# Splitting the turning of gathered rows between VectorE and TensorE, five column groups to three instead of four to four

## The reference

```python
def hmoe(x, p):
    """Two-level routing per token: top-1 expert group, then top-2 experts inside it."""
    t = x.reshape(bsz * L, D_MODEL)
    ...
    combine = jnp.einsum("tk,tke->te", gates,
                         jax.nn.one_hot(expert_id, N_EXPERTS, dtype=f32)).astype(x.dtype)
    out = jnp.zeros_like(t)
    for e in range(N_EXPERTS):
        hid = jax.nn.silu(t @ p["w_gate"][e]) * (t @ p["w_up"][e])
        out = out + (hid @ p["w_down"][e]) * combine[:, e:e + 1]
    return out.reshape(bsz, L, D_MODEL)
```

## Time and profile before

| | |
|---|---|
| median of 3 runs | 845.36 us (845.11 to 846.49) |
| the profiled execution | 845.81 us |
| span of the profiled execution, first to last instruction | 844.1 us |
| PE busy / PE weight loads busy | 789.7 / 647.9 us |
| DVE busy | 467.5 us (55%) |
| ACT busy / POOL busy | 204.4 / 104.5 us |
| mean granted TensorE clock | 0.976 of full speed |
| HBM read / written | 156.80 MB / 17.88 MB |

### The profile page before, as it was taken

The page is one execution under the profiler, slowest core; times in us unless marked ns, Lnnn a source line. Parts: engine busy times, 40 slices in busy tenths (PEclk is TensorE's granted clock), DMA queues, the critical chain, the costliest instruction groups (busy, mean ns, idle before and its releaser), DMA issues. The chain is left out here.

```text
span 844.1 us, 21325 instructions
## 1 busy us (share of the span) xinstructions
PE 789.7 (94%) x8993; PEld 647.9 (77%) x8993; DVE 467.5 (55%) x1092; ACT 204.4 (24%) x457; POOL 104.5 (12%) x169
## 2 busy tenths in 40 slices
PE   5999999999999999999999999698999999999935
PEld 3778877877888888777888888676778788788722
DVE  5999987236540242401223444756677777777726
ACT  5102325443211000102222211222222222222203
POOL 1000100113210000000000000122223223223100
PEclk9999999999999999999999989599999999999978
DMA  9531351131124900511021330799999999999745
GB/s 327 216 83 31 57 201 50 54 105 59 50 82 161 391 3 1 197 53 50 1 101 75 111 140 26 265 407 393 386 397 407 394 391 393 396 391 390 284 135 228
DMA packets 43654, 166.30 MB, mean 197 GB/s; under 512 B 16336, under 2 KB 21328, under 8 KB 26768
## 3 DMA queue, kind: packets, MB, share of 16 engines
q1 hardware_dynamic: 32912, 150.36, 47.1%
q0 software_dynamic: 6144, 9.45, 3.4%
q10 hardware_dynamic: 4544, 5.73, 1.9%
HBM read 156.80 MB, written 17.88 MB: 207 GB/s over the span
## 5 line engine op out<-in xcount | busy, mean ns | idle before, releaser
L876 PE MATMUL bank<-act_a,weight_ring 128*128 128x288 f32 x640 | 157.3, 406 | 0.5 <-ACT act_a L1436 0.5
L2300 DVE STREAM_TRANSPOSE region_t<-region_r 32x128 f32<-32x128 f32 x372 | 151.3, 407 | 6.8 <-DMA region_r<-ffn_rows,gather_now 0.7
L876 PEld LDWEIGHTS bank<-act_a,weight_ring 128*128 128x128 f32 x640 | 120.9, 190 | 33.3 <-ACT act_a L1436 0.6
L1164 PE MATMUL bank<-weight_ring,act_b 128*128 128x256 f32 x512 | 114.2, 385 | 0.0
L1164 PEld LDWEIGHTS bank<-weight_ring,act_b 128*128 128x128 f32 x512 | 98.5, 193 | 13.6
L1754 DVE TENSOR_TENSOR region_u<-region_u,bank 128x512 f32<-128x512 f32 (+1 forms) x26 | 17.9, 687 | 92.7 <-PE bank L1164 70.1
L1360 PE MATMUL bank<-region_t,weight_ring 128*64 128x80 f32 x1536 | 56.9, 233 | 1.9 <-issue 1.4
L1360 PEld LDWEIGHTS bank<-region_t,weight_ring 128*64 128x64 f32 x1536 | 54.6, 139 | 5.2 <-issue 4.5
L2262 DVE TENSOR_REDUCE score_max<-bank 128x2 f32<-128x512 f32 (+1 forms) x10 | 6.4, 637 | 65.3 <-PE bank L1204 61.5
L1360 PEld LDWEIGHTS bank<-region_t,region_g 128*64 128x64 f32 x1024 | 37.1, 138 | 6.6 <-issue 6.6
L1360 PE MATMUL bank<-region_t,region_g 128*64 128x80 f32 x1024 | 39.5, 234 | 2.7 <-issue 2.7
(11 more groups left out here) (355 smaller groups left out, 1178.8 us busy)
## 6 DMA issues: line engine op xcount, KB each, us to landing
weight_ring<-in_w_chunks SPq DMA_DIRECT2D x28, 1024.0 KB, 7.9
weight_ring<-in_w_up SPq DMA_DIRECT2D x17, 1024.0 KB, 11.8
weight_ring<-in_w_down SPq DMA_DIRECT2D x10, 1024.0 KB, 11.3
region_g<-in_w_up SPq DMA_DIRECT2D x8, 1024.0 KB, 12.2
region_g<-in_w_gate SPq DMA_DIRECT2D x8, 1024.0 KB, 9.7
conv_io<-in_w_gate SPq DMA_DIRECT2D x8, 1024.0 KB
conv_io<-in_w_down SPq DMA_DIRECT2D x8, 1024.0 KB, 11.5
weight_ring<-in_w_gate SPq DMA_DIRECT2D x7, 1024.0 KB
```

The lines of the kernel that those rows point to most:

```text
L876: m = pe.matmul(ps[:, 0:HALF], slot(c)[:, k, P * (mt % 2):P * (mt % 2 + 1)], x[:, k, HALF * h:HALF * (h + 1)], start=(k == 0), stop=(k == ...
L1164: m = pe.matmul(ps[0:L, CW * cc:CW * (cc + 1)], x[:, k, t0:t0 + L], slot(c)[:, k, :], start=(k == 0), stop=(k == KD - 1))
L2300: m = dve.transpose(xgT[b][DB * part:DB * (part + 1), 0:4, DB * blk:DB * (blk + 1)], xg[b][DB * blk:DB * (blk + 1), CW * part:CW * (part + 1)]
```

## The change

A constant `BY_DVE` takes the place of the fixed four: VectorE turns groups 0 to 4 and PE groups 5 to 7. The number of VectorE's instructions stays the same, each has five blocks instead of four; PE does three transposes instead of four for each expert, and ScalarE copies three groups. For the first expert PE still turns eight groups, three for ScalarE's copy and five for VectorE's.

```diff
+BY_DVE = 5
...
             def turn_x(pp, b):
 
                 pe.wait_ge(gathered[b], 16 * pp + 16)
-                for k in range(4):
-                    m = turn(banks[b][:, CAP * k:CAP * (k + 1)], xg[b][0:CAP, 4 + k::KD])
+                for k in range(KD - BY_DVE):
+                    m = turn(banks[b][:, CAP * k:CAP * (k + 1)], xg[b][0:CAP, BY_DVE + k::KD])
                 m.then_inc(turned_x, 1)
 
             def turn_first(pp, p):
 
                 turn_x(pp, 0)
-                for k in range(4):
+                for k in range(BY_DVE):
                     m = turn(banks[1][:, CAP * k:CAP * (k + 1)], xg[0][0:CAP, k::KD])
                 m.then_inc(first_turned, 1)
...
             def copy_x(pp, b):
 
                 act.wait_ge(turned_x, 2 * pp + (b + 1))
-                act.activation(xgT[b][:, 4:8, 0:CAP], banks[b][:, 0:4 * CAP].rearrange("p (k l) -> p k l", k=4), ACT.Copy)\
+                act.activation(xgT[b][:, BY_DVE:KD, 0:CAP],
+                               banks[b][:, 0:(KD - BY_DVE) * CAP].rearrange("p (k l) -> p k l", k=KD - BY_DVE), ACT.Copy)\
                     .then_inc(xT_act, 1)
...
                 for part in (2 * half, 2 * half + 1):
                     for blk in range(3):
                         m = dve.transpose(
-                            xgT[b][DB * part:DB * (part + 1), 0:4, DB * blk:DB * (blk + 1)],
+                            xgT[b][DB * part:DB * (part + 1), 0:BY_DVE, DB * blk:DB * (blk + 1)],
                             xg[b][DB * blk:DB * (blk + 1), CW * part:CW * (part + 1)]
-                            .rearrange("p (c k) -> p k c", k=KD)[:, 0:4])
+                            .rearrange("p (c k) -> p k c", k=KD)[:, 0:BY_DVE])
                 if half == 1:
                     m.then_inc(xT_dve, 1)
 
             def copy_first(p):
 
                 dve.wait_ge(first_turned, p + 1)
-                dve.tensor_copy(xgT[0][:, 0:4, 0:CAP], banks[1][:, 0:4 * CAP].rearrange("p (k l) -> p k l", k=4))\
+                dve.tensor_copy(xgT[0][:, 0:BY_DVE, 0:CAP],
+                                banks[1][:, 0:BY_DVE * CAP].rearrange("p (k l) -> p k l", k=BY_DVE))\
                     .then_inc(xT_dve, 1)
```

## The result

The changed kernel takes 851.39 us (median of 7 runs, 848.30 to 854.49), the kernel before 846.49 us (7 runs, 845.11 to 847.83): a ratio of 1.0058, 95% interval 1.0036 to 1.0080. It is slower, and by more than was forecast (847.8 us); the median lies 0.7 us above the range's upper end.

The account below looks back on a forecast made before the run. PE and its waits set the pace until 795 us, with DVE's turning path to become the bound; 3.0 + 0.08 - 0.68 = +2.4 us on the median of 845.36 gave 847.8 us (+0.28%), range 845.1 to 850.7.

Parts of the forecast that it names:

- What bounds the kernel: Expert stage: until 795 us PE and what it waits for set the pace, with a period of 7.91 us.
- 0.23 us of slack on DVE's: Between hidden product and next gate: DVE's path would allow the gate at 672.84, but it begins at 673.07.
- Its signs: Changed profile: turning 465 to 470 ns, distance 2.95 us, idle time labelled region_t, no in_w_up wait, period 8.04.
- The turning's 60 ns: DVE's turning instruction, 407 ns for 128 elements, takes 60 ns more for 160; six lie before the gate, 0.36 us.
- block nearly free: Rival on DVE's turning instruction: the extra block costs only 33 to 50 ns, time 845.4 to 846.4; chance 0.22.
- The first expert's +0.08 us: Ahead of the first gate: DVE's copy from PSUM is one group larger, +0.08 us.
- PE's transpose is worth 0.04 us: Before the down product: one transpose less gains 0.04 us, not 0.15, because PE then waits for the hidden product.
- So +0.13 us in 23 places, 3.0 us; in the seven others 2.95 is still under 3.08, nothing.: Hidden product to gate: 2.95 us instead of 2.82 in 23 places; the seven where PE's loop starts keep 3.08.
- - 0.68: Up product of expert 30: PE arrives 2.9 us later, so its 0.68 us delay for the weight goes away.
- The base: The kernel before: the forecast's +2.4 us was added to its median of 845.36 us.
- in proportion: Rival on DVE's turning: it grows by 80 to 102 ns and up, 854.4 us at 102 ns; chance 0.12.
- Faster through the transfers: Rival: PE reaches the 592 to 600 us transfer hole sooner, at most -0.7 us, if DVE's path doesn't bind; chance 0.06.

Follow-up runs that it names:

- seven to five: The change with DVE's twelve turning instructions dealt seven ahead of the hidden product and five behind it, instead of six and six: 845.83 us, ratio 0.9988.
- the two sizes of the experiments: The changed kernel with BY_DVE = 6 (860.94 us, 1.0180) and with BY_DVE = 3 (847.25 us, 1.0015).
- DVE's part alone: Against the kernel before, DVE turns five groups while PE still transposes four, group 4 left unread in the bank: 850.89 us, 1.0037.
- six groups: The changed kernel with BY_DVE = 6, so DVE turns six groups and PE two: 860.94 us, 1.0180 against the kernel before.
- filled end: Unread PE products added in the wait before the final sum; with 14, the kernel before takes 844.37 us, the change 848.01 us.
- 34 products: 34 unread PE products added in the wait before the final sum: the kernel before takes 861.35 us, the change 864.23 us.
- seven to five with 34: The change with turning dealt seven ahead and five behind, plus 34 unread PE products before the final sum: 862.07 us, 1.0173.
- eight to four: The change with DVE's turning instructions dealt eight ahead of the hidden product and four behind it: 849.70 us, 1.0032.

## Why the prediction was wrong, step by step

*What bounds the kernel.* Right. The distance from hidden product to gate is the longer of two paths, and 0.23 us of slack on DVE's was right: at five groups the gate follows the turning by 0.07 us, at four (with PE's transpose gone) and at seven to five it doesn't. Its signs came, but for two: the idle time ahead of the gate is labelled "issue" and not `region_t`, and the plain period is 8.07 us (671.18 to 679.25 from hidden product to hidden product) instead of 8.04.

*The turning's 60 ns.* Right: 467 ns. With the two sizes of the experiments it is 348, 407, 467 and 525 ns for three to six blocks, 59 ns for each, and some 170 ns that don't grow. These rows have 1.85 ns an element, nearly twice the 1.04 ns of plain work, with a source read at a stride of eight. The rival of a block nearly free, at 33 ns, is refuted. The Trainium skill, "Vector Engine (DVE) Microarchitecture Reference", section 3.8, has one element per cycle and lane in transposing; the measured instruction does not keep to that pace. Whether the stride is the reason was not tried.

*The first expert's +0.08 us.* Right for the copy, which takes 0.57 us instead of 0.49; in the time it can't be seen.

*PE's transpose is worth 0.04 us.* Right: 0.04 by the timeline, 1.1 us or nothing by the medians, and in the change not even that, since DVE is later (DVE's part alone takes as long as the whole).

*"So +0.13 us in 23 places, 3.0 us; in the seven others 2.95 is still under 3.08, nothing."* This is the step that failed, in its size: the 0.06 us between turning and gate were taken for every place. The seven loop starts stayed (but for one, with 3.17 instead of 3.08), and 16 places grew by 0.13 to 0.14. But seven of the 23, the fourth expert of each turn of the loop, grew by 0.25: 16 x 0.135 + 7 x 0.25 = 3.9 us. There the gate follows the turning by 0.19 us instead of 0.07. The kernel before could not show it: there PE wasn't waiting for DVE. DVE's part alone (3.07 to 3.08) and six groups (3.40 to 3.44, against 3.30) have it too, seven to five doesn't (2.78). With six groups the loop starts have it as well, so it goes with PE being released late by DVE at the last expert ahead of the loop's branch or the first one behind it; why it costs 0.12 us there is open.

The 22 experts from 6 to 28 give the size without the noise: +3.2 us. They hold 17 of the 23 places, for which the forecast had 17 x 0.13 = 2.2. Of the 1.0 that is missing 0.6 are the five fourth experts among them; the rest is small things: 0.1 at the loop starts, 0.1 in the plain places, and 0.2 between gate and hidden product (4.78 us instead of 4.77).

*"- 0.68" for the weight's wait.* The wait is gone in the changed kernel, as forecast. But it isn't a fixed property of the kernel before. Over five profiles of kernels with four groups on either engine it was 0.7, 0.6 and 0.3 us, and twice nothing. With the stall in the first experts, which also varies, one pair of profiles says little: the stage took 254.57, 254.17, 252.92 and 253.79 us in four profiles of the kernel before with and without filled end (mean 253.9), and 257.33, 257.37, 257.85 and 256.35 in four of the change alike (mean 257.2; the profile with 34 products, 259.47, is left out, see below). That is +3.4 us, against the forecast's 3.0 - 0.7 = 2.3. The difference is the seven fourth experts, 0.8, and the wait, which was on average smaller than 0.68 (0.3 over the five profiles).

*The base.* The forecast stood on 845.36 us, the median of three runs. The kernel before has had 846.49, 846.87, 845.75, 847.02 and 846.77 over 7 to 35 runs. Against the 846.8 of the two longest series the forecast of +2.4 would have read 849.2. The change has 850.4 to 851.4. So of the 3.6 us between forecast and result about 1.4 were the base, 1.1 the stage (3.4 against 2.3), and the rest is within the scatter of the medians.

*What the range left out.* The end. Nothing in the argument let it vary, and the profiles show 37.6 to 41.3 us for it. It did not decide the sign. Whether it adds to the median of the change is open: the profiles of the change are 848.9 to 849.7 us long and the two of the kernel before 844.1 and 842.6, a difference of 6.0, while medians differ by 3.6 to 4.9. The profiled executions of the kernel before, 845.81 and 844.36 us, lie in the lower half of its own spread (842.17 to 850.9 over 35 runs).

*The rivals.* "Nearly free" and "in proportion" fall by the 467 ns. "Faster through the transfers" had its condition right (DVE's path must not bind), and seven to five fulfils it: 0.9988 with the weight's wait back in the profile. By the interval it is still no gain over the kernel before.

## What to carry to other kernels

Between two engines that release each other, what counts is the slack of the path between one release and the next, in tenths of a microsecond, and not the busy share: in the change DVE was busy for 82% of the time and was the bound by six instructions, and at 87% (17.39 of 20 us) it no longer was when one of them had moved to its idle side. So when work is given to an engine, ask on which side of its own critical instruction it will lie, and re-divide it there: the count of instructions ahead and behind was worth 5 us here (850.80 to 845.83), as much as the change had cost and perhaps a little more; a gain over the kernel before is not shown. Here PE idled for some 15 us ahead of a last short stage, and 14 unread products in that wait kept its granted clock at 1.00 for the stage behind it, which brought the kernel before to 0.9972 of its time; they must end in time, as the 34 showed.

## What was not expected of the hardware

- **The granted clock in the middle of the stage.** Three profiles, of the change with 34 products, of seven to five with 34, and of eight to four, have a few microseconds around 595 to 605 us in which the granted clock is 0.66 to 0.94, and a gate 4.5 to 4.8 us after its hidden product instead of 3.08, 1.5 to 1.7 us lost. The first of them has another such gate at expert 3 (4.46 us). Of seven to five with 34 products:

```profile
595.00:600.00 5.00, 3.49 (x37) 2.17 (x40) 2.64 (x6) 0.37 (x1) 0.07 (x1) 0.73 0.99 356
600.00:605.00 5.00, 5.00 (x118) 3.95 (x112) 2.92 (x7) 1.65 (x4) 2.22 (x4) 0.93 1.04 388
```

  PE stands still for 1.5 of the first five microseconds. It does so in the changed kernel's profile too (busy for 3.26 of 5.00), and in the earlier trace rows, with the clock at 1.00. None of the six profiles with four groups on DVE shows the fall, and seven of the ten with five groups don't either; that is too few to say that it goes with five groups.
- **The spread of one program.** The same kernel on one core spreads over 6 to 9 us (35 runs of the kernel before: 842.17 to 850.9), with a mean granted clock between 0.967 and 0.979 over all runs of the two kernels. The first hidden product alone came between 550.3 and 553.4 us over all profiles. A difference of 0.3% needs a dozen runs of each.
- **A small fp32 transpose on PE** (80 x 80) costs 0.11 us when added to four, and gives 0.04 when taken from four, both as the path sees it.
